# The delta rule's triangles inverted by blocks of 64 on quadrants of the array, the two directions half a tile apart, and four gate tiles placed beside the last states

## The reference, cut to what matters

```python
def gated_delta_chunked(q, k, v, g, beta, s0):      # chunks of 64 tokens
    gc = jnp.cumsum(g, axis=-1)
    decay = jnp.where(incl, jnp.exp(jnp.where(incl, diff, 0.0)), 0.0)
    lmat = jnp.where(strict, jnp.einsum('bhncd,bhnsd->bhncs', kb, k) * decay, 0.0)
    rhs = jnp.concatenate([vb, kb * jnp.exp(gc)[..., None]], axis=-1)
    sol = lax.linalg.triangular_solve(lmat, rhs, left_side=True, lower=True, unit_diagonal=True)
    u, w = sol[..., :dv], sol[..., dv:]
    aqk = jnp.einsum('bhncd,bhnsd->bhncs', q, k) * decay
    def step(s, inp):
        v_new = ui - jnp.einsum('bhck,bhkv->bhcv', wi, s)
        o = jnp.einsum('bhck,bhkv->bhcv', qi * jnp.exp(gi)[..., None], s) + jnp.einsum('bhcs,bhsv->bhcv', ai, v_new)
        s = s * jnp.exp(glast)[..., None, None] + jnp.einsum('bhck,bhcv->bhkv', ki * jnp.exp(glast[..., None] - gi)[..., None], v_new)
        return s, o
```

## Time and profile before

| what | us |
|---|---|
| median of 3 runs (4388.75 to 4405.16) | 4392.58 |
| the profiled execution's own time | 4401.61 |
| its span in the trace | 4400.1 |
| TensorE busy | 3889.2 (88%) |
| VectorE, ScalarE, GpSimd busy | 1700.4, 1167.7, 1335.1 |
| mean granted TensorE clock, share of full | 0.92 |

### The profile page before, as it was taken

One profiled execution on the slowest core, in us unless ns is written; L12 is line 12 of the kernel. 1 busy time (PEld: TensorE's weight loads), 2 busy tenths in 40 slices (PEclk: granted clock), 3 DMA queues, 4 the chain that ended last, 5 costly groups with the idle time before them and its releaser, 6 DMA issues.

```text
span 4400.1 us, 71228 instructions
## 1 busy us (share of the span) xinstructions
PE 3889.2 (88%) x31216; PEld 2547.5 (58%) x31216; DVE 1700.4 (39%) x2886; ACT 1167.7 (27%) x2060; POOL 1335.1 (30%) x1150
## 2 busy tenths in 40 slices
PE   8997787788999989888899999798787888889998
PEld 3745787533444445555555555355566666657887
DVE  1343344213333321344323233412665555524444
ACT  2252111212111136333200000201455444522001
POOL 1401445000211211455333333200433333315444
PEclk9997888898888999999999999899898888999999
DMA  5420000431010121351121111221000000022222
GB/s 194 157 65 1 1 1 1 144 109 49 31 49 21 40 80 39 135 177 53 40 66 58 58 58 58 84 89 65 3 15 14 14 14 26 13 69 69 89 90 69
DMA packets 196270, 264.59 MB, mean 60 GB/s; under 512 B 6104, under 2 KB 149464, under 8 KB 193785
## 3 DMA queue, kind: packets, MB, share of 16 engines
q1 hardware_dynamic: 189024, 243.69, 16.7%
q10 hardware_dynamic: 6936, 16.35, 1.0%
HBM read 247.44 MB, written 12.58 MB: 59 GB/s over the span
## 4 chain that ended last, share of the span: by engine, by line
PE 75%; ACT 8%; DVE 7%; POOL 5%; issue 3%; DMA 2%; SPq 0%; ACTq 0%; DVEq 0%; POOLq 0%
PE ps L236 59%; PE ps L870 4%; PE ps L2749 2%; PE ps L742 2%; PE ps L467 1%; ACT mem L819 1%; PE ps L769 1%; PE ps L757 1%; DVE mem L1263 1%; DVE mem L2941 1%; PE ps L1878 1%; ACT mem L2684 1%; PE ps L476 1%; POOL mem L913 1%; DVE mem L800 1%
## 5 line engine op out<-in xcount | busy, mean ns | idle before, releaser
L236 PE MATMUL ps<-mem 64*64 64x64 f32 (+6 forms) x23680 | 2828.5, 314 | 210.4 <-ACT mem L644 35.7
L236 PEld LDWEIGHTS ps<-mem 64*64 64x64 f32 (+1 forms) x23680 | 1836.6, 160 | 1216.3 <-issue 689.4
L2652 POOL TENSOR_TENSOR mem<-mem 128x256 f32<-128x256 f32 (+1 forms) x192 | 182.4, 966 | 317.9 <-ACT mem L3085 182.1
L837 POOL TENSOR_SCALAR mem<-mem 128x768 f32<-128x768 f32 (+2 forms) x128 | 219.3, 1727 | 194.9 <-DVE mem L803 194.8
L870 PE MATMUL ps<-mem 128*128 128x128 f32 x1728 | 215.1, 287 | 45.9 <-POOL mem L913 45.9
L870 PEld LDWEIGHTS ps<-mem 128*128 128x128 f32 x1728 | 210.4, 202 | 48.4 <-DVE mem L1407 29.2
L574 POOL TENSOR_TENSOR mem<-mem 128x512 f32<-128x512 f32 (+1 forms) x72 | 74.8, 1057 | 454.4 <-ACT mem L569 453.1
L2094 POOL TENSOR_TENSOR mem<-mem 128x512 f32<-128x512 f32 (+1 forms) x68 | 84.9, 1248 | 389.0 <-PE ps L236 361.9
L2107 ACT ACTIVATE mem<-ps 128x384 f32<-128x384 f32 (+1 forms) x68 | 29.7, 438 | 642.3 <-PE ps L236 642.3
L2118 DVE TENSOR_TENSOR mem<-mem,ps 128x384 f32<-128x384 f32 (+1 forms) x68 | 33.3, 489 | 341.6 <-PE ps L236 341.6
L2749 PE MATMUL ps<-mem 128*128 128x128 f32 x816 | 146.4, 303 | 17.7 <-DVE mem L2674 17.1
(11 more groups left out here) (310 smaller groups left out, 4296.9 us busy)
## 6 DMA issues: line engine op xcount, KB each, us to landing
mem<-i_mod_w SPq DMA_DIRECT2D x48, 1024.0 KB, 6.9
...
```

Of the source, the lines that this page charges most:

```text
L236: ins = e.h.matmul(out, l, r, start=(i == 0), stop=(i == n - 1))
L837: K.pool.h.tensor_scalar(w, w, stat(i, o, 1), None, MUL).then_inc(*nm.up(tag, i, o))
L2652: K.pool.h.tensor_tensor(m3(self.slot(l)), self.lraw, bm(C(K, f"cm{self.d}", l, 64), 2 * self.np), MUL).then_inc(*self.mk.up(key, l))
```

## The change

1. `Inverse` is gone, with its table of masks, the DMA that loaded it and its 1792 columns. A unit now makes `Lc`, the two 64x64 blocks on the diagonal of each head's triangle (256 columns on 128 partitions), and `Lo`, the block off the diagonal. `Inverse64` inverts the diagonal blocks in levels 1 to 5. A **joining step** makes the off-diagonal block: a transpose of U, P = Lo times the beta-scaled U, then T times P, scaled into `ub`. DVE now does the scaling by beta, and the zero block of `ub` is set once by POOL.
2. The directions become lanes. `lane` runs the six units and chains of one direction back to back; lane 1 starts 8 steps behind lane 0, and a unit has 17 steps. The gate's first factor (`gates`) for the next unit is made near the end of the present one.
3. Four of the 8 gate tiles (`z_pe` and its like) start in the step in which lane 1's last chain starts. Lane 0's scratch lies in one ring slot only, and two weight slabs are fetched into the other two. `gate_and_out` does the other four.
4. `delta_norm` moves behind the fence, has four buffers, squares all heads first, and its result is awaited by the last four gate products.

```diff
-        return Inverse(K, ("dn", d, i), RI[d], d, h3(Lb[d]), lambda l: bm(K.lm[:, ...], 4), 4, 7, 7 * i)
+        return Inverse64(K, ("dn", d, i), ("dn", d, i - 1) if i else None, RI[d], d, d, m3(Lc[d]), 2, K.id64)
...
 def unit_pe(d, i):
-        yield from inverse(d, i).pe((a, b, c))
+        yield
+        yield
+        yield
+        inv = inverse(d, i)
+        yield from inv.pe(a)
+        vacant(K, c)
+        K.pe.wait_ge(*inv.u.at(inv.key, 5))
+        turn(K, K.ps[c], U, 0, 2).then_inc(*inv.pr.up(inv.key, "v", 6))
+        vacant(K, a)
+        K.pe.wait_ge(*ux.at(d, i, "ub", s))
+        for g in range(2):
+            for h in range(2):
+                ins = K.pe.h.matmul(K.ps[a][on(h), on(g)], Lo[d][on(s), w], part(ub[d][i % 2], s, s)[:, 2 * g + h, :], start=True, stop=True)
+        yield
+        claim(K, a, ux, d, i, "off")
+        K.pe.wait_ge(*inv.cp.at(inv.key, "P", 6))
+        for g in range(2):
+            for h in range(2):
+                ins = K.pe.h.matmul(K.ps[a + h][on(q), on(g)], T[on(h), ...], P[on(h), on(g)], start=True, stop=True)
+        yield
...
 def unit_dve(d, i):
-        K.dve.h.tensor_tensor(Lb[d], p[3 * d + 1], em[d], MUL).then_inc(*ux.up(d, i, "L"))
+        for e in range(2):
+            K.dve.h.tensor_tensor(m3(Lc[d])[on(e)], part(kk, e, e), part(em[d], e, e), MUL).then_inc(*ux.up(d, i, "L", e))
+        K.dve.h.tensor_tensor(m3(Lo[d])[on(s)], part(kk, s, q), part(em[d], s, q), MUL).then_inc(*ux.up(d, i, "L"))
...
+        for e in (s, q):
+            K.dve.h.tensor_tensor(part(ub[d][i % 2], e, e), m3(RI[d]["U"])[on(e)], strength(d, tt, on(e), 64), MUL).then_inc(*ux.up(d, i, "ub", e))
+        yield
+        K.dve.wait_ge(*inv.pr.at(inv.key, "u", 6))
+        K.dve.h.tensor_tensor(dst, src, be, MUL).then_inc(*ux.up(d, i, "off"))
...
-    def program(unit, chain):
-        for i in range(6):
-            run(unit(0, i), unit(1, i), *([chains(chain, i - 1)] if i else []))
-        run(chains(chain, 5))
-    end = [(scl, (d, 5, "ub")) for d in range(2)]
-    K.ring.lend(end, end, end)
+    def lane(unit, chain, d):
+        for _ in range(8 * d):
+            yield
+        for i in range(7):
+            yield from weave(*([unit(d, i)] if i < 6 else []), *([chain(d, i - 1)] if i else []))
...
+    for unit, chain, z in ((unit_pe, chain_pe, z_pe), (unit_dve, chain_dve, z_dve), (unit_act, chain_act, z_act), (unit_pool, chain_pool, z_pool)):
+        run(lane(unit, chain, 0), lane(unit, chain, 1), later(8 + 6 * 17, z()))
+    for m in range(0, 4, 2):
+        K.fetch(kn(256), wsrc(K.ins["e_w_in"], 3088 + m * 128, 256))
...
+    gn = delta_norm(K, ot, [K.alloc(512) for _ in range(4)])
-    rest = gate_and_out(K, "e", I["e_w_in"], (3088, 1024), I["e_w_out"], ot, sil, (hap, (lx, (1,))), mods, ALL[:7])
+    rest = gate_and_out(K, "e", I["e_w_in"], (3600, 512), I["e_w_out"], ot, sil, (hap, (lx, (1,))), mods, ALL[:7], 4, gn)
```

More of the change, by code:

```diff
@@ L1338, in delta_gates, with delta_scan @@
     dve()
-def delta_scan(K, OD, qT, kT, kt, vt, G, BE, GC, EGC, E2, EGL):
-    wm = [K.wmem[:, i * 512:(i + 1) * 512] for i in range(12)]
-    RI = [invert_memory(K, wm[5 * d:5 * d + 5]) for d in range(2)]
-    Lb = wm[10:12]
+def delta_scan(K, ot, hap, qT, kT, kt, vt, G, BE, GC, EGC, E2, EGL):
+    first = K.ring.fetched
+    held = K.ring.slots[K.ring.slot(first + 2)]
+    own = [[m[:, i * 256:(i + 1) * 256] for i in range(7)] for m in (held, K.alloc(1792))]
+    RI = [{"U": w[0], "T": w[1], "P": w[2], "Lm": w[3:5]} for w in own]
+    Lc, Lo, OD = [w[5] for w in own], [w[6] for w in own], ot[:, 4:8, :]
     gm, em, Rb, vn, v2, sd = ([K.alloc(512) for _ in range(2)] for _ in range(6))
@@ L1358, in delta_scan @@
     HS = [slice(h * 128, h * 128 + 128) for h in range(4)]
+    on = lambda e: slice(64 * e, 64 * e + 64)
+    part = lambda ap, r, c: h3(ap)[on(r), :, on(c)]
     def place(d, i):
@@ L1389, in unit_dve @@
         X, p = Xb[d][i % 2], K.ps
+        s, q = 1 - d, d
+        inv = inverse(d, i)
         K.dve.wait_ge(*pr.at(d, i, "gate"))
@@ L1430, in unit_pool @@
         K.pool.h.tensor_tensor(h3(gm[d]), bc(G[:, tt, 4 * d:4 * d + 4], 128), tri(d), MUL).then_inc(*gate.up(d, i))
+    def unit_pool(d, i):
+        tt, x, c0 = place(d, i)
+        X, inv = Xb[d][i % 2], inverse(d, i)
         K.pool.wait_ge(*ux.at(d, i, "x"))
@@ L1444, in unit_pool @@
             K.pool.h.tensor_tensor(h3(rt[d][i % 2]), h3(rt[d][i % 2]), tri(d), MUL).then_inc(*scl.up(d, i, "rt"))
-        yield
-        yield from inv
-        sig, key = inverse(d, i).done()
-        K.pool.wait_ge(*sig.at(*key))
-        if i >= 2:
-            K.pool.wait_ge(*ch.at(d, i - 2, "u"))
-        K.pool.h.tensor_tensor(h3(ub[d][i % 2]), h3(RI[d]["U"]), bc(BE[:, tt, 4 * d:4 * d + 4], 128), MUL).then_inc(*scl.up(d, i, "ub"))
+        for _ in range(10):
+            next(steps)
+            yield
+        if i < 5:
+            gates(d, i + 1)
+        yield
+        yield
     def product(bank, *terms):
@@ new lines, in z_pe, with z_act @@
+    def z_pe():
+        for m in range(4):
+            if m % 2 == 0:
+                n, w = K.take(kn(256))
+            vacant(K, m % 3)
+            group(K.pe, K.ps[m % 3], ((w[:, k, m % 2 * 128:m % 2 * 128 + 128], hap(k, 0, NX)) for k in range(KT)), KT).then_inc(*zl.up("ez0", m))
+            K.busy[m % 3] = [(zs, ("ez0", m))]
+            if m % 2:
+                K.spent(n, zl, "ez0", m)
+            yield
+    def z_act():
+        K.act.wait_ge(*ux.at(0, 5, "rt"))
+        for m in range(4):
+            K.act.wait_ge(*zl.at("ez0", m))
+            if m >= 2:
+                K.act.wait_ge(*zm.at("e", m - 2))
+            K.act.h.activation(Xb[0][m % 2], K.ps[m % 3], ACT.Silu).then_inc(*zs.up("ez0", m))
+            yield
@@ new lines, in z_dve, with z_pool, later @@
+    def z_dve():
+        for m in range(4):
+            K.dve.wait_ge(*zs.at("ez0", m))
+            K.dve.h.tensor_tensor(ot[:, m, :], ot[:, m, :], Xb[0][m % 2], MUL).then_inc(*zm.up("e", m))
+            yield
+    def z_pool():
+        for m in range(4):
+            yield
+    def later(n, g):
+        for _ in range(n):
+            yield
+        yield from g
+    for unit, chain, z in ((unit_pe, chain_pe, z_pe), (unit_dve, chain_dve, z_dve), (unit_act, chain_act, z_act), (unit_pool, chain_pool, z_pool)):
+        run(lane(unit, chain, 0), lane(unit, chain, 1), later(8 + 6 * 17, z()))
@@ L1571, in pe @@
             K.pe.wait_ge(*sq.at(h, 0))
-            K.pe.h.matmul(K.ps[b], C(K, "ones"), gm[h % 2], start=True, stop=True).then_inc(*sm.up(h))
-            K.busy[b] = [(sq, (h, 1))]
+            K.pe.h.matmul(K.ps[h], C(K, "ones"), gm[h], start=True, stop=True).then_inc(*sm.up(h))
+            K.busy[h] = [(sq, (h, 1))]
     def act():
```

206 lines of the change are left out of this document (67 added, 139 removed).

## The result

The changed kernel took **4267.48 us** (median of 4 runs, 4265.24 to 4272.22), the kernel before 4392.81 beside it: a ratio of 0.971, interval 0.969 to 0.973, so 125 us faster. The forecast was 4234 with a range of 4195 to 4295. The direction and the range held. The profiled execution took 4272.22 us, against a sum of 4243: the gain was 29 us smaller than forecast by the profiled executions, 33 by the medians.

The account below looks back on a forecast made before the run. TensorE's inverse and the head's latency bound the scan; 222.1 (halves) + 12.2 (last overlap) + 39.5 (end) + 6.0 (modulation, slab) + 24 (clock) = 303.8 against 462.4 us, 158.6 less, so 4234, range 4195 to 4295.

Parts of the forecast that it names:

- the bound: Old scan: the inverse is bound by TensorE's own work, 5.42 us per level; the head of a round is latency.
- A level of both lanes: New 64x64-block inverse: one level for both lanes costs 2.48 us at full clock, against 5.42 before.
- the layout of a half: From one lane's gate product to the other's: 21.2 us at full clock for a complete half, 14.6 of it TensorE.
- the 8 us for GpSimd beside it: VectorE's R beside GpSimd work: at 1.49 us instead of 0.7, ten halves would cost 8 us more, 4242.
- Clock +24, 2.2 us per half: TensorE clock 0.85 in the scan: a third of the loss hidden in waits, 2.2 us for each of eleven halves.
- The last unit and the overlap: Scan's end: a complete half of 21.2 us, then lane 1 finishing its tile beside lane 0's last chain, 12.2 us.
- The upper end of that term: Clock term: low clock lasts through the next head, every half starting slow, 5 us each, +55, giving 4265.
- The signs that were set down: Observations in the new scan listed beforehand as showing the forecast right, or wrong: halves over 28 us, over half at 1.2 GHz.
- Handovers: Rival: some 20 queue waits per half cost 0.15 us more each, +33 over eleven halves, 4267; chance 0.20.
- Full clock: Rival: TensorE's clock stays full in the scan, minus 24, 4210; chance 0.11.
- Array shapes: Rival: some 26 changes between 128x128 and 64x64 work cost 2.1 us per half, +24, 4258; chance 0.05.
- Lanes in turn: Rival: head waits block the other lane, a half becomes 36.0 us, 4425; chance 0.03 slower, 0.03 ending level.

Follow-up runs that it names:

- run 7: Changed kernel with both lanes in step (offset 0 instead of 8) and L and sd made one step earlier; 4198.84 us, ratio 0.955.
- 10: Changed kernel with lanes in step, L and sd one step earlier, and the whole norm inside the scan; 4199.35 us.
- the inverse alone: Changed kernel with lanes in step and all eight gate tiles and the old norm behind the scan, leaving only the 64-block inverse; 4252.49 us, ratio 0.968.
- Run 5: Changed kernel with two useless filling products on TensorE ahead of each tile's first inverse product; 4244.83 us, ratio 0.966.
- run 6: Changed kernel with VectorE making L one step earlier, ahead of the chain's work, and sd left in place; 4220.53 us, ratio 0.960.

## Why the prediction was right, and where its size was off

**Right: the bound, and what the inverse is worth.** A level of both lanes at 2.48 us came out at 2.48 to 2.49 in runs 7 and 10. By region the inverse alone gains 136.6 us, more than the whole change (129.0).

**Right: the layout of a half.** Gate, R, u, o, o's addition, L, scaling, sd, mask stand in the forecast order, with an idle 2.28 us where 2.4 stood. The pieces of 64 partitions took 0.42 us, not 0.35; R had a median of 0.69, so the 8 us for GpSimd beside it did not come. The four clears of `ub` took 0.48 us each and were over (416.30) before VectorE had formed the first exponent (416.46), so nothing came 1 to 2 us late. The last OD addition came at 712.9, not near 680: it carries 27 us that the next paragraphs account for.

**The term that was mis-sized: "Clock +24, 2.2 us per half".** The eleven halves took 244.6 us (413.59 to 658.19) against 222.9 forecast with it: 21.7 more, in three parts.
- The first half was laid out at half clock already, with 14.6 us, and took 17.2 at 0.50. These 2.6 us are the layout's and not the clock's.
- The next five were forecast at 13.7 + 2.2, twice 15.0 + 2.2 and twice 18.3 + 2.2, 91.3 in all, and took 104.3: 13.0 more. I had taken the clock from other scans at 0.85 to 0.87, and they had 0.66 to 0.73. Run 5 shows the clock's part: two of them took 16.2 and 16.4 us at 1.00 instead of 20.7 and 20.8. Against the 15.0 laid out, 1.2 to 1.4 us of each are not the clock's.
- The five complete ones took 123.0 instead of 117.0. Three of them had the very clock that I had assumed, 0.85, and still took 24.2 to 24.4 instead of 23.4, so here it is the price. R of k starts 5.9 us into the half (639.70) and 3.8 in run 6, whose gate product ran at full clock (585.97, 589.80). This alone is 2.1 of the 2.2, and the levels behind it run slow as well (0.82 from 649.50 on). That waits hide a third of the loss, which I had taken without a row for it, did not hold.

That the first six halves of run 5 took 106.7 us, close to the 105.9 forecast for them, is luck: they had a clock of 0.92.

The last unit and the overlap took 41.2 instead of 35.6 (clock 0.75), the end 41.9 instead of 39.5 (the four sums took 5.2 us, much of it at 1.2 GHz), the modulation steps 5.6 instead of 6.0. Together 21.7 + 5.6 + 2.4 - 0.4 = 29.3, the whole difference to 4243. The upper end of that term had stood in the text: every half starts slow, 4265. It did, in all of them, and the kernel took 4267. The Trainium skill ("TensorE: Matmul & The Clock Gate", HAM oscillation) describes waits that come back in each pass of a loop, after which each pass starts at the low clock. The trace agrees in the outcome, with 24 gate records of 1061 ns or more. Which wait brings the clock down is not shown: in run 6 the one before the first inverse product is gone, and the first seven halves still began slow.

**The signs that were set down.** Three came: one lane's gate products stood 48.8 us apart, sd stood between the scaling and the first mask, and TensorE idled at most 2.7 us at the sums. Two did not: the last OD addition, and the clock in the scan, 0.74 (413.59 to 699.42) where 0.8 to 0.9 stood. A clock of 0.74 means 52% of the time at 1.2 GHz, and "over half the scan at 1.2 GHz" stood there as a sign of being wrong. No half took over 25.3 us, where the other such sign stood at 28. The sign on a level, 2.3 to 2.8 us, I read in runs 7 and 10 alone. So the bound and the layout were right, and the view of the clock was not.

**The rivals.** *Handovers*, 4267, gives the right time, mostly for the wrong reason: u starts 0.06 us behind R's end (640.42 + 0.69, 641.17) and o 0.15 behind vn's, and run 5 shows that most of the time is the clock's. But its two halves at full clock took 1.2 to 1.4 us more than laid out, so handovers, changes of shape or the filling products have a part in it. *Full clock*: not in this kernel, but run 7's rounds ran so. *Array shapes*: a change costs something, but little here. At full clock two 128x128 instructions start at 639.27 and 639.38, 0.11 apart, and the first 64x64 one at 639.59, 0.20 behind. Back to 128x128 it is 0.15 (645.52, 645.67), where the next 64x64 group starts 0.04 behind the last. That is about 0.1 us per change, near the 0.08 of the prediction. But a complete half has 15 changes and not 26, most of them inside levels, whose 2.48 us hold them. Some five are left, which gives an estimate of 0.5 us per half at most, 6 in all instead of 24. *Lanes in turn* did not come in its full form. Its core did, and no step of the forecast priced the shift by itself. The step "one lane's head runs beside the other's levels" was laid out as an advantage and never set against lanes in step. In step, two heads overlap each other, and that was worth 7.7 us per round against 2.7.

**What beat both kernels.** Run 7: 4198.8 us, 69 less than the change, by two moved generator steps and no shift.
